# Attention: values' products in rows of eight key blocks, with eleven exponential tiles in place of eight

## The reference, cut to what matters

```python
def one_block(args):
    q_i, cq_i, blk = args
    s = jnp.einsum('bqhd,bkhd->bhqk', q_i, k).astype(jnp.float32) * ATTN_SCALE
    s = s + cq_i[..., :, None] - ck[:, :, None, :]
    q_pos = blk * Q_BLOCK + jnp.arange(Q_BLOCK)
    mask = key_pos[None, :] <= q_pos[:, None]
    p = jax.nn.softmax(jnp.where(mask, s, -jnp.inf), axis=-1)
    return jnp.einsum('bhqk,bkhd->bqhd', p.astype(v.dtype), v)
```

## Time and profile before

| | |
|---|---|
| median of three runs | 3209.83 us |
| the three runs | 3197.79 to 3213.23 us |
| the profiled execution | 3206.77 us |
| its span in the profile | 3205.2 us |
| TensorE (PE) busy | 2845.1 us, 89% |
| VectorE (DVE) busy | 1596.3 us, 50% |
| GpSimd (POOL) busy | 1380.8 us, 43% |
| ScalarE (ACT) busy | 1024.8 us, 32% |
| the visits' matmuls, L2069 | 1280, 558 ns each in the mean |
| row maxima, L2153 | 640, 608 ns |
| exponentials, L2121 | 640, 622 ns |
| adding to the sums, L1993 | 576, 1118 ns |

### The profile page before, as it was taken

How to read it: one execution, slowest core, us unless ns; L and a number is a source line. 1 busy time by engine, 2 the same in 40 slices (tenths; PEclk the granted TensorE clock), 3 DMA queues, 4 the chain that set the end, 5 groups by cost and what they waited for, 6 DMA issues and landing times. The chain is left out here.

```text
span 3205.2 us, 46929 instructions
## 1 busy us (share of the span) xinstructions
PE 2845.1 (89%) x17133; PEld 2257.1 (70%) x17133; DVE 1596.3 (50%) x2148; ACT 1024.8 (32%) x1721; POOL 1380.8 (43%) x986
## 2 busy tenths in 40 slices
PE   3887979695998999879999957999999999999999
PEld 2887878683674999879999954555555555554787
DVE  4222223234365579888555545455455555553432
ACT  4323232322245222212112212444444444544100
POOL 0000000001000477666988845766766777777000
PEclk9998989897999999989999986999999999999899
DMA  4101010104563688879777748877977877874532
GB/s 122 35 21 40 20 40 20 40 13 148 173 181 121 195 265 287 259 248 314 250 250 247 256 147 191 248 202 204 245 204 221 237 206 234 228 213 133 179 118 74
DMA packets 327904, 547.51 MB, mean 171 GB/s; under 512 B 76093, under 2 KB 220129, under 8 KB 319212
## 3 DMA queue, kind: packets, MB, share of 16 engines
q1 hardware_dynamic: 263564, 471.12, 49.9%
q10 hardware_dynamic: 61120, 58.83, 5.3%
q0 software_dynamic: 3008, 14.81, 1.3%
HBM read 449.58 MB, written 95.12 MB: 170 GB/s over the span
## 5 line engine op out<-in xcount | busy, mean ns | idle before, releaser
L1151 POOL TENSOR_TENSOR p_kp<-p_kp,p_qb 128x1024 f32<-128x1024 f32 x256 | 628.6, 2483 | 385.1 <-DMA p_kp<-in_cache_k_dram 305.3
L1993 POOL TENSOR_TENSOR at_acc<-at_acc,at_w 128x512 f32<-128x512 f32 (+3 forms) x576 | 644.0, 1118 | 250.8 <-ACT at_w L2121 186.2
L2153 DVE TENSOR_REDUCE at_mx<-at_mx 128x1 f32<-128x512 f32 (+3 forms) x640 | 382.8, 608 | 447.3 <-PE at_mx L2028 322.3
L112 PE MATMUL p_pb<-p_w,x_xh 128*128 128x256 f32 x2048 | 593.5, 290 | 8.1 <-DVE p_w L1465 8.0
L113 PE MATMUL p_pb<-p_w,x_xh 128*128 128x256 f32 x2048 | 580.8, 284 | 0.0
L114 PE MATMUL p_pb<-p_w,x_xl 128*128 128x256 f32 x2048 | 580.5, 283 | 0.0
L2121 ACT ACTIVATE at_w<-at_st,c_nckt 128x512 f32<-128x512 f32 (+3 forms) x640 | 390.0, 622 | 382.6 <-PE at_st L2054 195.8
L1567 DVE TENSOR_REDUCE p_sc<-p_kp 128x16 f32<-128x1024 f32 x256 | 307.5, 1214 | 219.9 <-POOL p_kp L1151 219.8
L112 PEld LDWEIGHTS p_pb<-p_w,x_xh 128*128 128x128 f32 x2048 | 392.4, 192 | 20.0 <-issue 11.0
L113 PEld LDWEIGHTS p_pb<-p_w,x_xh 128*128 128x128 f32 x2048 | 393.9, 192 | 0.0
L114 PEld LDWEIGHTS p_pb<-p_w,x_xl 128*128 128x128 f32 x2048 | 393.0, 192 | 0.0
(11 more groups left out here) (293 smaller groups left out, 3840.4 us busy)
## 6 DMA issues: line engine op xcount, KB each, us to landing
p_kp<-in_cache_k_dram SPq DMA_DIRECT2D x256, 512.0 KB, 4.9
at_vp<-in_cache_v_dram SPq DMA_DIRECT2D x256, 512.0 KB, 5.4
o_mt<-mixed SPq DMA_DIRECT2D x32, 512.0 KB, 5.4
p_raw<-in_w_in_dram SPq DMA_DIRECT2D x32, 512.0 KB, 7.2
at_q<-qh SPq DMA_DIRECT2D x32, 512.0 KB, 10.8
at_k<-kh SPq DMA_DIRECT2D x32, 512.0 KB, 8.5
l_raw<-in_w_in_dram SPq DMA_DIRECT2D x20, 512.0 KB
mixed<-l_w POOLq DMA_DIRECT2D x8, 1028.0 KB, 4.2
```

What stands on the lines that cost most here:

```text
L112: nc.tensor.matmul(out, lhs[0], rhs[0], start=(k == 0), stop=False)
L1151: nc.gpsimd.tensor_tensor(kp[:, g % 4], kp[:, g % 4], qb[:], ALU.mult).then_inc(kmul, 1)
L1993: nc.gpsimd.tensor_tensor(t[:, 512 - wd:512], t[:, 512 - wd:512], W[n % RW][:, 0:wd], ALU.add).then_inc(accd, 1)
L2153: nc.vector.reduce_max(mx[:, u % 2, j, seg:seg + 1], MX[r % 2][:, 0:wd], AX.X).then_inc(mread, 1)
```

## The change

The row length stays four, but a unit's first half of a pair of fours is held back until the second is ready, if the unit has eight blocks from there on; then both stand in a row. What is left over (the only four of a head's first unit, the last four of the third) goes as before. The number of tiles `RW` goes from 8 to 11.

```diff
-    RW = 8
+    RW = 11
...
                 if kb % G == G - 1:
                     pending.append((u, kb - G + 1, n - G + 1))
-                if pending and pending[0][2] + G - 1 <= n - 2:
-                    p = pending.pop(0)
+                ready = [p for p in pending if p[2] + G - 1 <= n - 2]
+                held = len(ready) == 1 and ready[0][1] % (2 * G) == 0 and ready[0][1] + G < blocks(ready[0][0])
+                for p in [] if held else ready:
+                    pending.remove(p)
                     weigh(p)
                     if p[1] == blocks(p[0]) - G:
                         later.setdefault(n + 4, []).append(("OF", p[0]))
```

## The result

| | before | after |
|---|---|---|
| median, same session | 3204.07 us | 3293.4 us (3291.1 to 3295.99) |
| profiled span | 3205.2 us | 3292.7 us |
| attention stage, granted clock | 0.97 | 0.91 |

The ratio is 1.0278, with a 95% interval from 1.0252 to 1.0304: 89 us slower. The forecast had the direction and the places right, but 42 us forecast against 89 measured lies outside its range.

The account below looks back on a forecast made before the run. TensorE was taken to set the pace, with VectorE next to no slack between visits. 3206.8 us + 32.4 (17.7 + 6.9 + 13.8 - 5.5 - 0.5) + 7 for the clock gave 3246 us, range 3214 to 3264.

Parts of the forecast that it names:

- What a visit costs, and what an appended one adds: TensorE's value products: a visit of four blocks costs 1.87 us, four appended 1.72; a lost visit saves 0.15 to 0.24.
- Step 17: Step (one key block's scores) 17, 15 heads: VectorE's gating exposed, 0.53 us won, 1.72 paid at step 21; +17.7 us in sum.
- Step 9, odd heads: Eight heads: gating of the unit before delays step 11's maximum product; 0.86 us won, 1.72 paid back; +6.9 us.
- Step 9, even heads: Eight heads: TensorE idles 2.5 us for VectorE's sample sum, nothing won, step 13 pays 1.72; +13.8 us.
- Steps 29 and 37: The 32 visits leaving these steps: nothing waits there, each saves 0.15 to 0.24 us; -5.5 us.
- The clock: Clock falls behind the even heads' new 2.5 us idle, bounds 0 and 13.6 us, half taken: +7 us.
- Savings without waits: Rival: lost visits save time and the waits don't come, 3192 to 3197 us; chance 0.10.
- Half of the waits: Rival: gating exposed but partly made good elsewhere, +5 to +20 us, 3212 to 3227 us; chance 0.13.
- Adder late: Rival: GpSimd lags over 8 us at a pair's end, exponentials wait for tiles, 3310 us and over; chance 0.04.
- The wait before L2087: Sign: TensorE's wait before the product needing the sample's sum, step 9 of even heads, should be 2.5 us.
- Half clock right behind the even heads' step 9: Sign: granted clock at half there, behind the new idle of TensorE; a fall was put at up to 1.7 us.
- no idle on ScalarE put down to GpSimd: Sign: with eleven tiles, ScalarE's exponentials should show no waiting for GpSimd to free a tile.

Follow-up runs that it names:

- `pairs_last`: The changed kernel with pairs only in the fourth unit of a head, none at steps 9 and 17: 3230.5 us, ratio 1.0083.
- `fill_all`: The changed kernel plus unused products: nine before the sample's-sum product, four in steps 11 (odd heads) and 19, ten in step 37 (odd heads): 3255.69 us.
- `pairs_last_fill`: `pairs_last` with eight more unused 512-wide products on TensorE in step 37 of each odd head: 3209.27 us, ratio 1.0004.
- `tiles11`: The kernel before with eleven exponential tiles in place of eight and nothing else: 3206.15 us, ratio 1.0003.
- `chosen`: The changed kernel without pairs in even heads' second unit and odd heads' last pair, gating moved where visits left, sum asked for in step 12: 3223.76 us.

## Why the prediction was wrong

- **What a visit costs, and what an appended one adds: right.** 1.87 and 1.71 us, forecast 1.87 and 1.72. The rule that changing the tiling mode drains TensorE (the Trainium skill, "TensorEngine Tiling (Array Packing)", section Tiling Modes) holds in direction: a lost visit saves 0.15 us here, and 0.29 in step 37 of odd heads, where no other product of the samples stands behind it (forecast 0.15 to 0.24).
- **Step 17: right.** 0.54 us won and 1.71 paid back, +1.17, forecast +1.19.
- **Step 9, odd heads: right.** From step 9's to step 12's scores 3.09 us (2316.12 to 2319.21), where it took 3.89: 0.80 won, 0.86 forecast.
- **Step 9, even heads: right.** Idle 2.43 us, nothing won (the step after it begins 0.44 us behind the product, 0.25 before the change: the clock is already at 0.50 there).
- **Steps 29 and 37: right in the products, wrong in what they do.** In the steps at full clock `pairs_last` saves 5.6 us, forecast 5.5. That "nothing waits" was taken for "nothing can be lost" is the first error: `pairs_last` loses 26 us.
- **The clock: the term that was mis-sized.** The step that failed reads "A fall costs up to 3.4 / 2 = 1.7 us, less where TensorE then waits for VectorE anyway. Bounds 0 and 8 x 1.7 = 13.6". Forecast +7, found 50 to 60. It was wrong in three ways. It allowed falls only behind the eight idle stretches, while they also come behind idle stretches of 1 us (steps 11 and 19) and with no idle at all (steps 35 to 37). It took a fall's length from stages where dense work followed at once; in the changed kernel's stage it lasts 6.8 to 10.2 us, once 17. And it did not see what the visits do for the clock: each of them left for a place four steps later, and where a thin place lay in front of it, that place got longer. That products put into these places shorten the falls or take them away is shown for the two places that were filled alone, and for all of them together by `fill_all`; what it is about them that the clock goes by is not shown.
- **Rivals.** Savings without waits: excluded, the waits are there. Half of the waits: excluded. Adder late: without effect on the time, but nearer than forecast. The forecast took 1.05 us a block, the mean over all widths; the 512-wide additions (L1993, 384 of them) take 1.31 us each and begin 1.42 us apart, so in a unit's wide blocks GpSimd is at the 1.4 us that the forecast named for this rival, and ScalarE is released by it at 2300.42, 0.04 us behind the end of the scores.
- **The signs named.** The wait before L2087, the one of about 1 us at steps 11 and 19, and the 3.6 us visit (3.58 at steps 21 and 33; 3.15 where it holds diagonal blocks) came as said. "Half clock right behind the even heads' step 9" came as well, three times as long. The sign "no idle on ScalarE put down to GpSimd" did not: the list puts 16.8 us down to it, of which TensorE felt nothing.

The sum with what was measured: 34 us (waits, less savings) + 50 to 55 us (clock) = 84 to 89 us; by the second count, in the profiled stage, it is 28 + 56 = 84.

Open is what exactly decides between a fall and none at equal places of equal heads, and why the recovery takes from 3.4 to 10.2 us.

## What to carry to other kernels

When dense work is gathered into longer rows, look at the thin stretches that it leaves, not only for waits but for what TensorE does there: products of one column count as busy in the profile, and here the clock fell 1 us behind 1.84 us of them. Before moving a visit, list for both ends what is late next: the work that another engine did in its cover (here 1.6 us of gating and a 2 us sum) is exposed. A mean over mixed widths hides a margin: 1.05 us a block was 1.42 in the wide ones. And a test that costs little: put useless products into the suspected gap; if the kernel gets faster and the granted clock rises, the clock was part of the loss. Look at the other places too, since falls went where nothing had been added.

## What the runs showed of the hardware that was not expected

- The granted clock fell to 0.50 for 10.2 us while TensorE was busy in 5.60 of the 5.60 us ahead of it. The Trainium skill, "TensorE: Matmul & The Clock Gate", section Part 1, ties the clock to how busy the engine has been; in these rows the profile's busy time does not tell a fall beforehand.
- 64 useless products made a kernel 21 us faster (`pairs_last` 3230.5, `pairs_last_fill` 3209.27 us), and 248 made the changed one 38 us faster (3293.4 and 3255.69; by the ratios 41).
- The same pattern of two heads, eight times in a row, has falls in some repetitions and none in others, and not in the same ones in `before` and `tiles11`. 1.15 us more work a repetition made `chosen` 9 us faster (3223.76 and 3214.77 us).
